# One start column per row for z and h in the last feed-forward part of a two-layer fp32 backbone

## The reference

```python
def swiglu(z, w_in, w_out):
    gate, up = jnp.split(z @ w_in, 2, axis=-1)      # w_in 1024 x 5632
    return (jax.nn.silu(gate) * up) @ w_out         # w_out 2816 x 1024

        h = h + 0.5 * m[8] * swiglu(modulate(rmsnorm(h, ffn2_norm_g[l]), m[6], m[7]),
                                    ffn2_w_in[l], ffn2_w_out[l])
        if not last:
            hc = hc + ...                            # the same for the context tokens
    return rmsnorm(h, final_norm_g)
```

## Time and profile before

| | us |
|---|---|
| median of 3 runs | 1570.7 |
| the three runs | 1564.53, 1570.7, 1571.11 |
| the profiled execution, device time | 1571.65 |
| its span | 1569.9 |
| TensorE busy | 1550.9 (99%) |
| last feed-forward part at L446, 1512 matmuls | 178.17 |

### The profile page before, as it was taken

The page is one execution under the profiler, slowest core; times in us unless marked ns, Lnnn a source line. Parts: engine busy times, 40 slices in busy tenths (PEclk is TensorE's granted clock), DMA queues, the critical chain, the costliest instruction groups (busy, mean ns, idle before and its releaser), DMA issues.

```text
span 1569.9 us, 22187 instructions
## 1 busy us (share of the span) xinstructions
PE 1550.9 (99%) x8796; PEld 1339.8 (85%) x8796; DVE 1054.0 (67%) x1305; ACT 682.6 (43%) x1112; POOL 159.1 (10%) x193
## 2 busy tenths in 40 slices
PE   8999999999999999999999999999999999999997
PEld 6888888889888988888888898888888897999997
DVE  5777874794868567874378477784368578965553
ACT  4434433333784343433233353343332369654452
POOL 0011110022100201110002200011002211000011
PEclk9999999999999999999999999999999999999999
DMA  9577664665322257663367446764367523465562
GB/s 367 198 212 206 201 186 137 206 203 129 107 81 80 82 188 208 199 186 98 121 205 212 114 153 190 217 197 115 98 203 229 154 89 127 135 201 187 188 200 82
DMA packets 79468, 262.53 MB, mean 167 GB/s; under 512 B 13201, under 2 KB 13457, under 8 KB 78353
## 3 DMA queue, kind: packets, MB, share of 16 engines
q1 hardware_dynamic: 71696, 248.70, 49.3%
q0 software_dynamic: 7680, 12.59, 5.0%
HBM read 247.62 MB, written 1.05 MB: 158 GB/s over the span
## 4 chain that ended last, share of the span: by engine, by line
PE 94%; DVE 2%; ACT 1%; DMA 1%; issue 0%; SPq 0%; POOL 0%; POOLq 0%; DVEq 0%; ACTq 0%
PE bank L446 84%; PE bank L568 2%; PE bank L574 2%; PE bank L570 2%; DMA ada_head<-head_w 1%; PE bank L737 1%; PE bank L711 1%; PE bank L709 1%; PE bank L710 1%; PE bank L523 0%; PE bank L739 0%; DVE w_lo L1173 0%; PE bank L462 0%; PE bank L454 0%; DVE l_q L1441 0%
## 5 line engine op out<-in xcount | busy, mean ns | idle before, releaser
L867 ACT ACTIVATE w_hi<-raw 128x1024 fp32r<-128x1024 f32 x317 | 335.9, 1060 | 722.1 <-PE bank L446 707.1
L1173 DVE TENSOR_TENSOR w_lo<-raw,w_hi 128x1024 fp32r<-128x1024 f32 x317 | 388.3, 1226 | 313.3 <-ACT w_hi L867 312.8
L446 PE MATMUL bank<-z_hi,w_hi 128*128 128x512 f32 (+1 forms) x1480 | 537.7, 363 | 1.8 <-DVE w_lo L1173 1.4
L446 PE MATMUL bank<-z_lo,w_hi 128*128 128x512 f32 (+1 forms) x1480 | 534.7, 361 | 0.0
L446 PE MATMUL bank<-z_hi,w_lo 128*128 128x512 f32 (+1 forms) x1480 | 534.5, 361 | 0.0
L446 PEld LDWEIGHTS bank<-z_hi,w_hi 128*128 128x128 f32 x1480 | 278.5, 188 | 46.0 <-DVE w_lo L1173 1.8
L446 PEld LDWEIGHTS bank<-z_hi,w_lo 128*128 128x128 f32 x1480 | 279.8, 189 | 42.4
L446 PEld LDWEIGHTS bank<-z_lo,w_hi 128*128 128x128 f32 x1480 | 278.4, 188 | 42.8 <-issue 1.0
L446 PE MATMUL bank<-h_hi,w_hi 128*128 128x512 f32 (+1 forms) x770 | 267.4, 347 | 0.0
L446 PE MATMUL bank<-h_hi,w_lo 128*128 128x512 f32 (+1 forms) x770 | 266.9, 347 | 0.0
L446 PE MATMUL bank<-h_lo,w_hi 128*128 128x512 f32 (+1 forms) x770 | 266.9, 347 | 0.0
(11 more groups left out here) (187 smaller groups left out, 1405.6 us busy)
## 6 DMA issues: line engine op xcount, KB each, us to landing
raw<-weights SPq DMA_DIRECT2D x320, 512.0 KB, 4.1
ada_raw<-ada_w SPq DMA_DIRECT2D x128, 512.0 KB, 4.3
ada_head<-head_w SPq DMA_DIRECT2D x8, 1024.0 KB, 19.1
up_acc<-up_acc POOLq DMA_DIRECT2D x20, 256.0 KB, 6.5
down_acc<-down_acc POOLq DMA_DIRECT2D x12, 256.0 KB, 6.2
up_acc<-up_acc POOLq DMA_DIRECT2D x40, 64.0 KB, 6.1
res<-x_t SPq DMA_DIRECT2D x4, 512.0 KB, 5.1
down_acc<-down_acc POOLq DMA_DIRECT2D x24, 64.0 KB, 5.5
```

The costliest lines, as they stand in the source:

```text
L446: m = pe.matmul(bank[:, to], w, x[:, k, at], start=start and i == 0, stop=stop and i == 2, skip_group_check=True)
L867: act.activation(w_hi[:, r, :], raw[:, r, :], ACT.Copy).then_inc(hi_ready, 1)
L1173: dve.tensor_tensor(w_lo[:, r, :], raw[:, r, :], w_hi[:, r, :].bitcast(F32), ALU.subtract).then_inc(lo_ready, 1)
```

## The change

The one start column gives way to two tables. `Z_FIRST` has rows 0 to 3 of z at column 112 as before and rows 4 to 7 at column 120. `H_FIRST` has rows 0 to 20 of h by threes at columns 8, 24, 40, 56, 72, 88 and 104, and row 21 at 112 as before.

```diff
-LAT0 = 112
+Z_FIRST = [112] * 4 + [120] * 4
+H_FIRST = [8 + 16 * (k // 3) for k in range(KF - 1)] + [112]
...
-        ALONE = (COLS[0], slice(LAT0, LAT0 + SEQ))
-
-        def all_of(n_streams):
-            return BOTH if n_streams == 2 else ALONE
+
+        def alone(first, k):
+            return slice(first[k], first[k] + SEQ)
+
+        def all_of(n_streams, first, k):
+            return BOTH if n_streams == 2 else (COLS[0], alone(first, k))
...
-        def row_cols(n, s):
-
-            return COLS[s] if streams(dft(n)) == 2 else ALONE[1]
+        def row_cols(n, s, k):
+
+            return COLS[s] if streams(dft(n)) == 2 else alone(Z_FIRST, k)
...
-                        m = product(pa[q], k, q, z_hi, z_lo, k, part, k == 0, k == KD - 1)
+                        m = product(pa[q], k, q, z_hi, z_lo, k, all_of(streams(dft(n)), Z_FIRST, k), k == 0, k == KD - 1)
...
-                            m = product(po[dd % 2], b, q % RING, h_hi, h_lo, k, all_of(len(ss)), k == 0, k == KF - 1)
+                            m = product(po[dd % 2], b, q % RING, h_hi, h_lo, k, all_of(len(ss), H_FIRST, k), k == 0, k == KF - 1)
```

More of the change, by code:

```diff
@@ L561, in row @@
                     c = slice(k * P, (k + 1) * P)
-                    z = row_cols(n, s)
+                    z = row_cols(n, s, k)
                     last = k == KD - 1 and s == both
@@ L579, in first_slots @@
                 if not both:
-                    z = row_cols(n, 0)
                     pe.wait_ge(hi_ready, base + 3)
                     for k in range(KD):
+                        z = row_cols(n, 0, k)
                         row(k, 0, (0, 1))
@@ L589, in first_slots @@
                     for k in range(KD):
-                        m = pe.matmul(banks[2][:, COLS[0]], w_lo[:, 2, k * P:(k + 1) * P], z_hi[:, k, z], start=False,
+                        m = pe.matmul(banks[2][:, COLS[0]], w_lo[:, 2, k * P:(k + 1) * P], z_hi[:, k, row_cols(n, 0, k)], start=False,
                                       stop=(k == KD - 1), skip_group_check=True)
@@ L610, in up_stage @@
                 n = 3 * l + 2 * f
-                part = all_of(streams(dft(n)))
                 def slot(i, p):
@@ L914, in z_high @@
                     act.wait_ge(zt_ready, z_piece(n, k, s))
-                    act.activation(z_hi[:, k, row_cols(n, s)], scr[:, k % 3, COLS[s]], ACT.Identity,
+                    act.activation(z_hi[:, k, row_cols(n, s, k)], scr[:, k % 3, COLS[s]], ACT.Identity,
                                    bias=n_shift[:, n, k, s:s + 1]).then_inc(z_hi_ready, 1)
@@ L990, in up_stage @@
                         act.wait_ge(hid_ready, HID0 + 1 + j)
-                        act.activation(h_hi[:, jj, all_of(streams(w))[1]], scr[:, 2, 0:w], ACT.Copy).then_inc(hid_hi_ready, 1)
+                        act.activation(h_hi[:, jj, all_of(streams(w), H_FIRST, jj)[1]], scr[:, 2, 0:w], ACT.Copy).then_inc(hid_hi_ready, 1)
                     ring_acts(at, t)
@@ L1282, in z_low @@
                     dve.wait_ge(z_hi_ready, z_piece(n, k, s))
[L1283 to L1284 removed]
+                    dve.scalar_tensor_tensor(z_lo[:, k, row_cols(n, s, k)], scr[:, k % 3, COLS[s]], n_shift[:, n, k, s:s + 1],
+                                             z_hi[:, k, row_cols(n, s, k)].bitcast(F32), ALU.add, ALU.subtract).then_inc(z_ready, 1)
                 def head_turn(b):
@@ L1380, in slot @@
                         hid = slice(jj, jj + 1) if isinstance(jj, int) else bass.ds(jj, 1)
-                        dve.tensor_tensor(h_lo[:, hid, all_of(streams(w))[1]].rearrange("p a n -> p (a n)"), scr[:, 2, 0:w],
-                                          h_hi[:, hid, all_of(streams(w))[1]].rearrange("p a n -> p (a n)").bitcast(F32),
+                        dve.tensor_tensor(h_lo[:, hid, all_of(streams(w), H_FIRST, jj)[1]].rearrange("p a n -> p (a n)"), scr[:, 2, 0:w],
+                                          h_hi[:, hid, all_of(streams(w), H_FIRST, jj)[1]].rearrange("p a n -> p (a n)").bitcast(F32),
                                           ALU.subtract).then_inc(hid_lo_ready, 1)
```

## The result

| | before | after |
|---|---|---|
| median of 18 runs each, us | 1564.88 | 1571.55 |
| lowest and highest | 1563.70, 1571.11 | 1570.99, 1573.56 |
| the profiled execution, device time | 1571.65 | 1571.72 |

A forecast was written before the change was run, and what follows sets the result against it. The prediction took TensorE's 117.8 ns matmul cadence to bound the kernel. From the profiled 1571.65 us it subtracted 1584 x 4.45 ns (7.0 us), other terms 0, giving 1564.6 us (chance 0.42), range 1561 to 1575.

The forecast's parts named there:

- What bounds the kernel: Last part: TensorE bounds it, 1512 matmuls at L446 in 178.17 us; their 117.8 ns alone moves the end.
- The three runs read as two cadences: Three runs of before: two at 117.8 ns, one at 113.3; 1584 matmuls at 4.45 ns make 7.0 us.
- The choice: z and h matmuls: weight and moving streams collide, repeating after 512 bytes; one clean meeting gives 6.7 ns gap, 113.3 ns.
- z rows at 120: Half of z's 1056 matmuls (528), at L446 and in first slots: -4.45 to +2.2 ns each.
- z rows left at 112: z rows 0 to 3, unmoved: expected to take the good cadence through the disturbance twice in a slot.
- h rows at the table's columns: 504 of h's 528 matmuls at new columns: -4.45 to +2.2 ns each, one meeting expected nearly everywhere.
- 152 changes of start: Row-to-row column changes, 88 in slots and 64 in output rows: at most 1.5 us, at least a gain, taken 0.
- writers: ACT and DVE writing z and h at other columns: taken as 0, covered by their 65 and 82 us waits.
- The disturbance that should help: z slots: two column changes in each should flip 117.8 to 113.3 ns and make the good cadence hold.
- Slower: the new starts collide twice: 1032 matmuls at new columns: 1574 to 1576.6 us, chance 0.11; full 6.7 ns step, 1578.5 us, chance 0.06.
- Nothing changes: Whole kernel: the 11.1 ns gap does not depend on start column; 1571 us (1570.7 to 1571.65), chance 0.20.
- The two rules of the Trainium skill: TensorE never waits on other memory users; weight loading takes no read bandwidth: start column worth nothing, 1571.65 us.

The follow-up runs named there:

- peel_only: Kernel before with four slots written out ahead of the loop, nothing added: eight runs at 1563.81 to 1564.88 us, four at 1570.47 to 1571.03.
- same_place: Kernel before with z rows 4 to 7 at column 48, h by threes at 48 and 112: eight runs 1563.73 to 1564.50 us, four 1570.77 to 1571.93.
- z_only: Changed kernel with all h rows back at column 112, z rows as changed: 5 runs, 1570.77 to 1572.22 us, median 1571.4.
- kick: Kernel before plus a small unused matmul ahead of each of 41 slots and each output row, 49 in all: 7 runs, 1576.60 to 1577.75 us.
- steps_64: Changed kernel with z rows at 112 and 96, h by threes at 0, 16, 32 to 96, last at 112: 5 runs, 1570.15 to 1572.52 us.
- all_120: Changed kernel with every row of z and h at column 120: 5 runs, 1571.39 to 1572.60 us.
- z116_h108: One column per table, all z rows at 116 and all h rows at 108, against 112 before: 10 runs, 1572.92 to 1574.48 us.
- z8_h24: One column per table, all z rows at 8 and all h rows at 24, against 112 before: one execution, 1572.16 us.
- kick_few_again: The kernel of kick_few repeated in another batch: 12 runs, 1564.70 to 1565.58 us, ratio to before 0.9974.
- kick_few: Kernel before, four slots written out, small matmuls at three places only (two in up stage, one ahead of down stage): 12 runs, 1564.31 to 1565.46 us.
- same_place_kick: The columns of same_place with the three small matmuls of kick_few: 12 runs, 1564.62 to 1565.97 us, median 1564.98.

## Why the prediction was wrong, point by point

**What bounds the kernel** was right: TensorE alone, the writers' waits unchanged, every ns of the 1512 matmuls one for one in the time.

**The three runs read as two cadences** was right, as far as traces go: 178.17 us in before and 171.59 in peel_only, the same code but for four slots written out. The step came out at 6.6 us and not 7.0, because the 72 matmuls of the first slots give nothing. But "two of three" was read as the kernel's habit. Of 18 runs 12 were good, of all 106 runs in the five rows of the table above 61. The profiled execution, against which the sum was made, belongs with the 45 others. So the gain of 7.0 us was counted against a group that the kernel is mostly not in, and the most that the change could have brought to the median of 18 was next to nothing. The right sum has two base lines: from the lower group there is everything to lose, from the upper one 6.6 us to gain.

**The step that failed: "The choice".** It took the 113.3 ns for what a clean meeting of two streams costs anywhere but at an edge, with places repeating after 512 bytes. Measured, they repeat after 256, and of ten places the good cadence was seen at one, the one that the change leaves. The terms had their bounds right and their value wrong (ns for each matmul, against 117.8):

| term | taken | bounds | measured |
|---|---|---|---|
| z rows at 120 | -4.45 ns | -4.45 to +2.2 | 118.4, +0.6 |
| z rows left at 112 | -4.45 ns | none given | 117.7, none |
| h rows at the table's columns | -4.45 ns | -4.45 to +2.2 | 118.5, +0.7 |
| 152 changes of start | 0 | a gain to +1.5 us | none between equal places (same_place) |
| writers | 0 | | 0 |

Against the profiled execution of before the measured sum is small: 0.6 us more in the chain's piece, and 0.07 us in the device time. Against a good execution it is 178.75 - 171.59 = 7.2 us; the piece starts 0.3 us earlier after (1377.65 us against 1377.97 in peel_only), and the device times of these two executions differ by 6.84 us. The medians are 6.67 us apart. The rows left at 112 have a part in this. The prediction counted on the good cadence for them too, on account of the changes of start; measured against a good execution they lose 4.4 ns for each matmul, although nothing of theirs was moved, because the rows at 120 end the good cadence and rows 0 to 3 did not find it again by themselves. The trace of z_only has one such moment: its first slot at L449 settles into the good cadence, starts 113 and 114 ns apart up to the end of row 3, goes bad in row 4, and no later slot is good.

**The disturbance that should help** was half right. Interruptions do set the cadence, to good behind 48 of the 49 in kick. A change of column can do it too, from 96 to 112 in every slot of steps_64. But those of the changed kernel did not: from 120 back to 112 its z rows stayed at 117.7 ns in every slot.

**The rivals.** "Slower: the new starts collide twice" had the sign, and not the mechanism. Its condition (a row that begins in the middle of a 64-byte piece) is not what decides, since columns 0, 16, 32 and 96 begin at the head of such a piece and lose too. And it took the price from 117.8 up, 2.3 to 6.9 us, where the loss is that of the good cadence, from 113.3 up. "Nothing changes" is what the two profiles say, and a study of these two traces alone would have ended there. The two rules of the Trainium skill that the prediction draws on (page "SBUF — State Buffer", section "Who interferes with whom", and page "TensorE: Matmul & The Clock Gate", Part 2) do not speak of a start column, and as the prediction read them every one would be equal. By all_120, z116_h108 and z8_h24, with nothing changed but that column, they are not: z ran at 118.3, 119.2 and 116.7 ns, h at 118.3, 119.4 and 120.1.

**What stays open.** Why the place 48 of 64 columns, and of those tried only it, has a second cadence; what in an execution makes the stream good or bad at a restart (0.20 us brought the good one in kick_few_again, 0.21 us the bad one in before), and why that share differs from batch to batch. The weight blocks never moved, so whether a row's place counts by itself or by its distance from a weight block is not told apart. No run here shows the memory's inside. The small matmul differs from its neighbours in width, weights and address at once, and I have not tried which of these sets the cadence.

## What to carry to other kernels

When a few runs of a kernel lie in groups, find out which group the profiled execution belongs to before making a sum against it, and ask what the change does to either group. A stream of matmuls that each load new weights can have more than one stable cadence at the same address, so an operand's start column is worth measuring one column at a time, all rows on one column, and it is no proof for a neighbour 16 bytes away. If a kernel has a good and a bad cadence, a few interruptions of 0.25 us each at the head of the long stretch can be cheaper than hoping: here three took away the upper group, at a price of 0.4 us in the lower one.

## What the runs showed of the hardware that I had not expected

Matmuls of 256 fp32r columns with a LDWEIGHTS each, at 2.4 GHz, followed one another in 113.3 to 120.1 ns when nothing but the moving operand's start within 256 bytes was changed, and 16 bytes to either side of the best place cost some 6 ns against its good cadence (z116_h108). At the best place two cadences, 113.3 and 117.8 ns, each held for over 170 us (peel_only, before). With three small matmuls in between, all 36 executions of kick_few, its repetition and same_place_kick had the lower one.
